# Low parts of the value compression's first-layer weights made by GpSimd instead of VectorE

## The reference

```python
def _compress(k, pos_emb, w1, w2):
    ch = k.reshape(B, n_chunk, 16, N_KV, HEAD_DIM)
    first  = einsum('bcsgd,sdh->bcgh', ch + pos_emb[:16], w1[:16])
    second = einsum('bcsgd,sdh->bcgh', ch + pos_emb[16:], w1[16:])
    hid = silu(first[:, :-1] + second[:, 1:])
    return einsum('bngh,hd->bngd', hid, w2)
```

## Time and profile before

| | |
|---|---|
| median of 3 runs | 2296.21 us (2295.29 to 2299.93) |
| the profiled execution | 2295.55 us, its span 2293.8 us |
| PE busy | 2187.5 us (95%) |
| DVE busy | 1465.0 us (64%) |
| ACT busy | 1010.4 us (44%) |
| POOL busy | 220.2 us (10%) |

### The profile page before, as it was taken

One profiled execution on the slowest core, in us unless ns is written; L12 is line 12 of the kernel. 1 busy time (PEld: TensorE's weight loads), 2 busy tenths in 40 slices (PEclk: granted clock), 3 DMA queues, 4 the chain that ended last, 5 costly groups with the idle time before them and its releaser, 6 DMA issues.

```text
span 2293.8 us, 46100 instructions
## 1 busy us (share of the span) xinstructions
PE 2187.5 (95%) x17635; PEld 1955.1 (85%) x17635; DVE 1465.0 (64%) x2978; ACT 1010.4 (44%) x1932; POOL 220.2 (10%) x357
## 2 busy tenths in 40 slices
PE   8999999999999899899999999999999998997997
PEld 8999999999988445489999999999998974544997
DVE  5888564567776666654478875545677756666544
ACT  5333333535644566523243333344446445565232
POOL 0000000000000333300000000000000002334000
PEclk9999999999999999999999999999999999999999
DMA  6655486835220876843345644777142236778421
GB/s 226 191 156 156 117 221 164 203 94 182 98 74 18 135 125 111 204 137 104 101 144 156 189 125 133 220 187 206 35 173 93 74 59 108 111 124 215 150 93 40
DMA packets 405540, 312.69 MB, mean 136 GB/s; under 512 B 224282, under 2 KB 376282, under 8 KB 404041
## 3 DMA queue, kind: packets, MB, share of 16 engines
q1 hardware_dynamic: 399752, 268.70, 46.5%
q0 software_dynamic: 5568, 41.05, 5.0%
HBM read 282.80 MB, written 77.09 MB: 157 GB/s over the span
## 4 chain that ended last, share of the span: by engine, by line
PE 76%; DVE 11%; ACT 3%; DMA 2%; DVEq 2%; issue 2%; POOL 2%; SPq 1%; ACTq 0%; POOLq 0%
PE ps L1001 30%; PE ps L989 10%; PE ps L1182 6%; PE ps L1261 5%; PE ps L1282 3%; PE ps L1420 3%; PE ps L1408 3%; PE ps L1444 2%; PE ps L1207 2%; PE ps L1542 2%; POOL pr L931 2%; DMA w_raw<-in_w_in 1%; PE ps L1695 1%; PE ps L1176 1%; PE ps L1550 1%
## 5 line engine op out<-in xcount | busy, mean ns | idle before, releaser
L454 DVE TENSOR_TENSOR wL<-w_raw,wH 128x2048 fp32r<-128x2048 f32 (+1 forms) x77 | 176.9, 2298 | 112.3 <-ACT wH L448 112.1
L1001 PE MATMUL ps<-hH,wH 128*128 128x272 f32 x1088 | 226.0, 289 | 1.5 <-DVE wL L454 1.3
L1001 PE MATMUL ps<-hH,wL 128*128 128x272 f32 x1088 | 226.2, 289 | 0.0
L1001 PE MATMUL ps<-hL,wH 128*128 128x272 f32 x1088 | 224.8, 288 | 0.0
L931 POOL TENSOR_SCALAR pr<-pr,inv,zg 128x512 f32<-128x512 f32 (+3 forms) x256 | 156.6, 621 | 549.3 <-DVE inv L3001 549.3
L473 ACT ACTIVATE wpH<-w_raw 128x512 fp32r<-128x512 f32 x168 | 102.0, 623 | 175.8 <-DMA w_raw<-in_w_in 106.1
L1001 PEld LDWEIGHTS ps<-hH,wH 128*128 128x128 f32 x1088 | 171.3, 189 | 3.5 <-DVE wL L454 3.4
L1001 PEld LDWEIGHTS ps<-hH,wL 128*128 128x128 f32 x1088 | 170.9, 189 | 0.0
L1001 PEld LDWEIGHTS ps<-hL,wH 128*128 128x128 f32 x1088 | 170.6, 188 | 0.0
L1420 PEld LDWEIGHTS ps<-con,pr 128*128 128x128 f32 x640 | 69.7, 144 | 107.2 <-POOL pr L931 90.0
L448 ACT ACTIVATE wH<-w_raw 128x2048 fp32r<-128x2048 f32 (+1 forms) x77 | 147.6, 1917 | 21.2 <-DMA w_raw<-in_w_in 16.4
(11 more groups left out here) (425 smaller groups left out, 5860.3 us busy)
## 6 DMA issues: line engine op xcount, KB each, us to landing
w_raw<-in_w_in SPq DMA_DIRECT2D x59, 1024.0 KB
rows_keep<-in_cache_kv SPq DMA_DIRECT2D x256, 128.0 KB, 3.4
craw<-rows_keep SPq DMA_DIRECT2D x32, 1024.0 KB, 7.4
w_raw<-in_w_in SPq DMA_DIRECT2D x64, 256.0 KB
k_sel<-in_cache_kv SPq DMA_DIRECT2D x128, 128.0 KB, 4.9
v_sel<-in_cache_kv SPq DMA_DIRECT2D x128, 128.0 KB, 8.2
out_new_win_sample<-in_state_win POOLq DMA_DIRECT2D x16, 1016.0 KB, 5.3
w_raw<-in_w_out_a SPq DMA_DIRECT2D x8, 1024.0 KB
```

Of the source, the lines that this page charges most:

```text
L454: dve.tensor_tensor(block_part(wL, b), block_part(w_raw, b), block_part(wH, b).bitcast(F32), ALU.subtract).then_inc(w_lo, 1)
L1001: last = nc.tensor.matmul(ps[:, bank + hf, 0:HALF], st, x[:, k, hf * HALF:(hf + 1) * HALF], start=k == 0 and w is wH and x is xH, stop=k = ...
```

## The change

The four `w1_low(1, j)` of each layer leave DVE's list, and POOL makes the same low parts right after its four weight DMAs. PE now waits for them on a semaphore that POOL counts (`po_step`, which also takes over the counting of the scaled probabilities), and DVE's `w1_sum(1, j)`, which overwrites half of the raw quarter, waits for the low part of that quarter. The counts of the other semaphores are adjusted to it.

```diff
@@ orders and counts
-                     "low 1 0", "low 1 1", "low 1 2", "low 1 3", "sum 1 0", "joint 1 0", "sum 1 1", ...
+                     "sum 1 0", "joint 1 0", "sum 1 1", ...
+        def value_low(l, j):
+            return (UNITS + 4) * l + j + 1
+        def scaled(l, i):
+            return (UNITS + 4) * l + 4 + i + 1
@@ POOL, after the weight DMAs
+                for j in range(4):
+                    pool.wait_ge(w1_hi, w1_act(l, "high", 1, j))
+                    pool.tensor_tensor(w1L[j][:], w1_raw[:, j:16:4, :], w1H[j][:].bitcast(F32), ALU.subtract).then_inc(po_step, 1)
@@ POOL, scaling of probabilities
-                    last.then_inc(pa_sc, 1)
+                    last.then_inc(po_step, 1)
@@ PE, prompt_layer
-                    pe.wait_ge(w1_lo, w1_dve(l, "low", n // 5, j))
+                    if n:
+                        pe.wait_ge(po_step, value_low(l, j))
+                    else:
+                        pe.wait_ge(w1_lo, w1_dve(l, "low", 0, j))
@@ PE, turn
-                    pe.wait_ge(pa_sc, UNITS * l + i + 1)
+                    pe.wait_ge(po_step, scaled(l, i))
@@ DVE, w1_sum
+                    if kv:
+                        dve.wait_ge(po_step, value_low(l, j))
@@ DVE, order of work
                 unit_start(4)
-                w1_low(1, 0)
                 chunk_parts(4, 3)
                 dve.wait_ge(kv_out, 160 * l + 160)
                 prompts_low(5, 0)
                 chunk_sum(6, 0)
                 prompts_low(5, 1)
-                w1_low(1, 1)
-                w1_low(1, 2)
                 prompts_low(5, 2)
-                w1_low(1, 3)
                 prompts_low(5, 3)
```

More of the change, by code:

```diff
@@ L381, in build @@
         pa_ctev = [sem("pa_ctev_act"), sem("pa_ctev_dve")]
-        pa_s, pa_nm, pa_exp, pa_inv, pa_sc = sem("pa_s"), sem("pa_nm"), sem("pa_exp"), sem("pa_inv"), sem("pa_sc")
+        pa_s, pa_nm, pa_exp, pa_inv, po_step = sem("pa_s"), sem("pa_nm"), sem("pa_exp"), sem("pa_inv"), sem("po_step")
         pa_t, pa_ta, pa_td = sem("pa_t"), sem("pa_ta"), sem("pa_td")
@@ L599, in build @@
         W1_BY_DVE = ["low 0 0", "sum 0 0", "low 0 1", "sum 0 1", "low 0 2", "low 0 3", "joint 0 0", "joint 0 1", "sum 0 2", "joint 0 2", "sum 0 3", "joint 0 3",
-                     "low 1 0", "low 1 1", "low 1 2", "low 1 3", "sum 1 0", "joint 1 0", "sum 1 1", "joint 1 1", "sum 1 2", "joint 1 2", "sum 1 3", "joint 1 3"]
+                     "sum 1 0", "joint 1 0", "sum 1 1", "joint 1 1", "sum 1 2", "joint 1 2", "sum 1 3", "joint 1 3"]
         def w1_act(l, what, kv, j):
```

## The result

The changed kernel is slower. Its median is 2304.21 us (2297.93 to 2312.3, 11 runs), against 2298.57 us (2292.51 to 2302.45, 11 runs) for the kernel before on the same chip. The ratio is 1.0035 (95% interval 1.002 to 1.005). The medians lie 5.6 us apart; 2299.8 us was predicted.

The account below looks back on a forecast made before the run. Mostly PE's own work bounds the kernel, but DVE's program, with ACT close behind, decides one stretch per layer. Removal 0, port loss 2 x 1.8 = 3.6 us on the median 2296.21 gave 2299.8 us, range 2295.4 to 2302.5.

Parts of the forecast that it names:

- What bounds the stretch, and what the removal brings: At DVE's prompt part 3, ACT's half is late next, so removing four subtractions brings 0 to -0.1 us a layer.
- Duration on POOL: Each subtraction moved to POOL takes 2.35 us, the middle of 2.15 to 2.53 us.
- The shared port: POOL's subtractions and DVE's two-SBUF-input pieces in parts 2 and 3 block each other; 1.8 us lost a layer.
- 3d - 5.2: General formula for the port loss in us per layer, d being the duration of one POOL subtraction.
- the one named as the alternative: POOL slips in between two pieces of DVE's part 2; same work in another order, with the same end.
- step 4: In layer 0, DVE's part 3, ready at 633.81, waits until 635.74 and ends at 637.34 against 635.55; loss 1.8 us.
- PE's new waits: PE's waits for POOL's low parts ahead of the prompt's parts cost nothing.
- POOL's configuration change: At 618.3, ahead of the first subtraction: 0 in the sum, under 1 us in layer 0 if quarter 0 comes late.
- PE's clock: Up to the next joint product, slack of 1.80 and 0.49 us; taken as 0, bound 0 to 1.5 us a layer.
- The sum: Over two layers, 2 x 1.8 = 3.6 us; 2299.8 us against the median, 0.16% more.
- Clearly slower: Quarters 1 to 3 ahead of part 3: slower POOL subtraction; at 3.0 us each, 3.8 us a layer, 2303.8 us; 24%.
- a clock loss added to the forecast: Remark inside the 24% rival: a PE clock loss on top also leads to the slower side; no size of its own.

Follow-up runs that it names:

- no_lows: Changed kernel without POOL's subtractions, the semaphore only counted and the value weights' low parts left out; 2297.04 us, ratio 0.9998 to the kernel before.
- write_only: Changed kernel with POOL's subtractions replaced by zero-filling memsets of about equal length that read nothing from SBUF; 2295.0 us against 2298.37 for the kernel before.
- late3: Changed kernel, but POOL starts quarter 3's subtraction only after DVE has ended prompt part 3; 2298.89 us, ratio 1.0002 to the kernel before.
- after_b: Changed kernel without edit, its third profile (one execution); no median given, idle ahead of the joint product 3.12 and 3.13 us.
- gap2_fill: Changed kernel plus 24 PE matmuls a layer ahead of prompt part 2, in PE's long idle; 2301.48 us against 2296.33 for the kernel before.
- filler: Changed kernel plus 24 unread PE matmuls a layer in the wait ahead of unit 6's joint product; 2300.07 us, ratio 1.0011 to the kernel before.
- gap_fill: Changed kernel plus 32 PE matmuls ahead of prompt part 3, missing the long idle ahead of part 2; 2306.22 us against 2297.36 for the kernel before.
- before_b: Kernel before, without edit, profiled a second time; no median given, idle ahead of the joint product 3.12 and 1.76 us.
- halves_first: Against the changed kernel: ACT's part 3 half before rounding quarter 3, DVE keeps quarters 1 and 2, POOL's quarter 3 after part 3; 2300.15 us against 2298.37 before.
- dve_delay: Changed kernel without POOL's subtractions; DVE makes quarter 3's low part twice between prompt parts 2 and 3; 2303.15 us against 2298.37 for the kernel before.
- experiment 7: Further single profiles without edit, one of the kernel before and two of the changed kernel; no medians given.

## Why the prediction was wrong

- **What bounds the stretch, and what the removal brings: right.** 0 to -0.1 us a layer was said; no_lows shows -0.05 (A 8.32 and 8.35 against a mean of 8.39), with ACT's half late next.
- **Duration on POOL: right.** 2.35 us taken, 2.41 measured.
- **The shared port: right in kind and nearly in size.** 3d - 5.2 with d = 2.41 gives 2.0 us a layer; 1.58 was measured, 1.8 forecast. The order was the one named as the alternative: POOL slipped in between two pieces of part 2. The end isn't quite the same: one piece (0.38 us) had passed between POOL's second and third subtraction, work that my step 4 put behind POOL's last. That the port is the cause is shown by write_only against the changed kernel; that the subtraction for quarter 3, in a row with the two others, makes it cost, by late3.
- **PE's new waits at 0, POOL's configuration change at 0: right in cost.** PE does wait for POOL now and then (0.44 us ahead of part 1 in layer 0 of after_b), but write_only has even later arrivals and no loss; the change ran at 621.5 us and the first subtraction started at 621.60 with its usual 2.42 us.
- **The step that failed: PE's clock.** "PE's work up to the next joint product has slack of 1.80 and 0.49 us, so I take 0 and keep 0 to 1.5 us a layer." Measured: 1.02 us a layer on average, nothing in three layers of eight, 1.2 to 2.6 in the five others. I had read the slack as something that a slower PE would use up. The runs show the reverse: the long idle ahead of part 2 moves the first fall earlier, the clock is back about 8 to 12 us ahead of the joint product (4 to 7 in the three layers of the kernel before in which it fell), the slack grows to 2.36 to 3.13 us, and behind it the clock may fall again, on work that nothing hides. gap2_fill shows it by taking the long idle away (six of six layers at 5.65 or 5.66). filler fills the second idle and agrees, but with two layers only. Open is whether the early fall also makes the second likelier at a given idle: behind waits of 2.31 us and more the clock fell in 10 of 14 layers with a long idle ahead of part 2 (changed kernel and gap_fill), in 1 of 4 without (before_b, write_only, late3, halves_first).
- **The sum.** 3.6 us predicted, 3.1 measured for what the sum contained (2 x (1.58 - 0.06)), 5.1 with the clock. Of the 4.4 us between 2299.8 and 2304.21, 2.4 are the kernel before itself, which had a median of 2298.57 in this comparison against the 2296.21 of the three runs that I started from. The other 2.0 equal the clock term (2 x 1.02), but partly by luck: the port took 0.5 less than predicted, and 0.5 us of the medians' difference lies outside the stretch. The range ended at 2302.5. Either shift alone would have stayed inside it (2302.2 or 2301.8), both together didn't. The clock's own bound of 1.5 us a layer, put on top of the sum, would have reached 2302.8, still 1.4 us short.
- **The rivals.** "Clearly slower" has the right side and the wrong mechanism: POOL's subtraction was not slower than its rows, but "a clock loss added to the forecast leads to the same side" is what happened. It deserved a price and a chance of its own.

Open: the profiled execution of the changed kernel is 8 us above its own median. It was already 3.2 us behind at the first mark (620.72 us against 617.55), before anything changed, so part of that is not the change's; some 5 us more came between the stretch of layer 0 and that of layer 1. From the start of ACT's first rounding in layer 0 to that in layer 1 this execution took 1141.4 us, the three others of the changed kernel 1132.6 to 1137.4, the two of the kernel before 1133.6 and 1138.6; what varies there stays open. And dve_delay's medians differ by 2 us more than its stretch explains, which its interval allows.

## What to carry to other kernels

An engine that takes over work shares ports with the one relieved: look for instructions of the other with two SBUF operands that run beside it, and count the moved instructions in a row, since each of them can hold up a short piece for nearly its full length (here 2.38 us recorded instead of 0.38). When PE gets one long wait in place of several short ones, price the clock behind every later wait too, by the nearest row at the low level (here 1.2 us for the joint product; the stretch behind it lost 1.2 to 2.6), and give it a chance of its own. A slow stretch that lies over hidden work costs nothing, and moving it off that work makes it cost.

## What the runs showed of the hardware

- The port is passed on at instruction ends, and one waiting instruction gets in. Around the end of POOL's second subtraction one DVE piece of 0.38 us came through, then POOL had the port again, although DVE's next piece was ready. In all eight layers of the changed kernel the first piece is recorded with 1.18 to 1.24 us and the second with 2.33 to 2.38; POOL lost almost nothing by it (three subtractions of 2.41 us in 7.17 us).
- The clock didn't fall behind any of the 17 waits ahead of the joint product that were 0.34 to 1.80 us long, over all kernels here; of the 18 that were 2.31 to 3.13 us it fell behind 11. PE's last work before the wait was eight chunk transposes (1.03 or 1.04 us) wherever it was read, and no run varied that. The same idle (3.12 and 3.13 us in one profile) gave both. So the price is a chance, and one profile can't show it: the changed kernel had 1.2 and 1.4 us of loss in one profile and, per layer, 2.6 and 0 in another. The Trainium skill (TensorE: Matmul & The Clock Gate, section "What's actually happening") says that the hardware's watch on PE's activity runs freely and doesn't start with the kernel, so that the same kernel meets it at different points; the pair of rows in experiment 7 is consistent with it, though no run here shows that watch itself.
